# Down projection of a gated conv FFN: the loop over row blocks moved outside the loop over feature slices

## The reference

```
def conv_ffn(x, w_up, conv_w, conv_b, w_down):
    s_len = x.shape[1]
    u = x @ w_up                                        # 1024 -> 2 * 3072
    up = jnp.pad(u, ((0, 0), (CONV_W - 1, 0), (0, 0)))  # causal, width 3
    c = conv_b + sum(up[:, j:j + s_len] * conv_w[j] for j in range(CONV_W))
    gte, val = c[..., :D_FF], c[..., D_FF:]
    return (jax.nn.gelu(gte) * val) @ w_down            # 3072 -> 1024
...
x = layer_norm(ALPHA * x + ffn, ln2_g[l], ln2_b[l])
```

## Time and profile before

| what | value |
|---|---|
| median of 3 runs | 3718.81 us |
| the profiled execution's own time | 3718.81 us |
| its span, first to last instruction | 3716.7 us |
| TensorE (PE) busy | 3423.7 us, 92% |
| VectorE (DVE) busy | 2533.5 us, 68% |
| ScalarE (ACT) busy | 1644.5 us, 44% |
| GpSimd (POOL) busy | 652.1 us, 18% |
| mean granted TensorE clock | 0.964 of full speed |

### The profile page before, as it was taken

One profiled execution on the slowest core, in us unless ns is written; L12 is line 12 of the kernel. 1 busy time (PEld: TensorE's weight loads), 2 busy tenths in 40 slices (PEclk: granted clock), 3 DMA queues, 4 the chain that ended last, 5 costly groups with the idle time before them and its releaser, 6 DMA issues. The chain is left out here.

```text
span 3716.7 us, 40502 instructions
## 1 busy us (share of the span) xinstructions
PE 3423.7 (92%) x15012; PEld 2715.9 (73%) x15064; DVE 2533.5 (68%) x4093; ACT 1644.5 (44%) x2025; POOL 652.1 (18%) x367
## 2 busy tenths in 40 slices
PE   7999899947888999978999799999999999999997
PEld 5788777835555666656777588888888888888886
DVE  5899999967766767636555465567566756666665
ACT  5767777225566666654221133333333333333331
POOL 1022222323455555660000000000000000000000
PEclk9999999978899999999999899999999999999999
DMA  6223322352211111007443433323322333323230
GB/s 166 47 90 102 102 97 90 121 143 53 59 47 44 49 37 44 16 23 238 159 159 102 131 111 116 102 91 123 113 96 102 106 124 102 102 82 114 102 100 33
DMA packets 233022, 356.88 MB, mean 96 GB/s; under 512 B 43453, under 2 KB 150605, under 8 KB 218814
## 3 DMA queue, kind: packets, MB, share of 16 engines
q1 hardware_dynamic: 231774, 349.95, 30.5%
q0 software_dynamic: 1056, 4.36, 0.3%
HBM read 290.13 MB, written 64.13 MB: 95 GB/s over the span
## 5 line engine op out<-in xcount | busy, mean ns | idle before, releaser
L88 PE MATMUL ffn_up<-ffn_xh,ffn_uh 128*128 128x512 f32 x1536 | 599.4, 390 | 9.4 <-DVE ffn_ul L1561 9.4
L90 PE MATMUL ffn_up<-ffn_xh,ffn_ul 128*128 128x512 f32 x1536 | 599.0, 390 | 0.0
L89 PE MATMUL ffn_up<-ffn_xl,ffn_uh 128*128 128x512 f32 x1536 | 598.9, 390 | 0.0
L1519 ACT ACTIVATE ffn_c<-ffn_up,ffn_cb,ffn_cw 128x512 f32<-128x512 f32 x192 | 148.8, 777 | 766.0 <-PE ffn_up L90 760.3
L810 POOL TENSOR_TENSOR att_plo<-att_pf,att_phi 128x1024 fp32r<-128x1024 f32 x168 | 407.7, 2428 | 389.7 <-ACT att_phi L870 389.5
L88 PE MATMUL frt_acc<-frt_xh,frt_wh 128*128 128x512 f32 x864 | 339.6, 393 | 20.3 <-issue 9.4
L88 PEld LDWEIGHTS ffn_up<-ffn_xh,ffn_uh 128*128 128x128 f32 x1536 | 289.2, 188 | 70.6 <-issue 5.2
L89 PE MATMUL frt_acc<-frt_xl,frt_wh 128*128 128x512 f32 x864 | 337.9, 391 | 0.0
L90 PE MATMUL frt_acc<-frt_xh,frt_wl 128*128 128x512 f32 x864 | 337.8, 391 | 0.0
L89 PEld LDWEIGHTS ffn_up<-ffn_xl,ffn_uh 128*128 128x128 f32 x1536 | 289.3, 188 | 59.9
L90 PEld LDWEIGHTS ffn_up<-ffn_xh,ffn_ul 128*128 128x128 f32 x1536 | 289.1, 188 | 60.1
(11 more groups left out here) (267 smaller groups left out, 7482.8 us busy)
## 6 DMA issues: line engine op xcount, KB each, us to landing
ffn_ur<-in_w_up_dram SPq DMA_DIRECT2D x96, 1024.0 KB, 4.8
ffn_dr<-in_w_down_dram SPq DMA_DIRECT2D x64, 768.0 KB, 4.4
zt<-frt_out SPq DMA_DIRECT2D x108, 256.0 KB, 4.3
frt_wr<-in_w_main_dram SPq DMA_DIRECT2D x51, 512.0 KB, 4.2
att_raw<-zt SPq DMA_DIRECT2D x64, 256.0 KB, 4.1
mrg_sg<-zt SPq DMA_DIRECT2D x64, 256.0 KB, 3.6
frt_xr<-in_xt_dram SPq DMA_DIRECT2D x12, 1024.0 KB, 7.8
yt<-att_y SPq DMA_DIRECT2D x32, 256.0 KB, 2.3
```

Of the source, the lines that this page charges most:

```text
L88: pe.matmul(out, ahi, bhi, start=first, stop=False)
L89: pe.matmul(out, ahi, blo, start=False, stop=False)
L90: return pe.matmul(out, alo, bhi, start=False, stop=last)
L1519: act.activation(c[:, k % 2, a, :], up[:, k % 2, a, :], ACT.Identity, scale=cw[:, 2, a, k % NS:k % NS + 1], bias=cb[:, a, k % NS:k % NS + ...
```

## The change

In `fall`, the loop over the four row blocks `b` becomes the outer loop and the loop over the three slices `i` the inner one. The same 36 matmuls are issued, with the same operands and into the same banks, but a bank now gets its nine matmuls in one run. Before, each slice was waited for just before its twelve matmuls. Now one wait for all three slices (`hs` up to `G * (j + 1)`) stands ahead of the first matmul. The wait for the freed bank (`da`) stays ahead of each bank's first matmul, and the count of `dm` after each bank's last one.

```
                 pe.wait_ge(S["dsd"], p + 1)
-                for i in range(G):
-                    pe.wait_ge(S["hs"], G * j + i + 1)
-                    sl = (G * j + i) % R
-                    for b in range(TB):
-                        if p and i == 0:
-                            pe.wait_ge(S["da"], TB * (p - 1) + b + 1)
+                pe.wait_ge(S["hs"], G * (j + 1))
+                for b in range(TB):
+                    if p:
+                        pe.wait_ge(S["da"], TB * (p - 1) + b + 1)
+                    for i in range(G):
+                        sl = (G * j + i) % R
                         last = split3(pe, dn[:, b, :], hh[:, sl, b * P:(b + 1) * P], hl[:, sl, b * P:(b + 1) * P],
                                       dh[:, ch, i, :], dl[:, ch, i, :], i == 0, i == G - 1)
-                        if i == G - 1:
-                            last.then_inc(S["dm"], 1)
+                    last.then_inc(S["dm"], 1)
```

## The result

| | before | changed |
|---|---|---|
| median of 6 runs, us | 3718.35 | 3743.16 |
| lowest to highest, us | 3716.21 to 3719.37 | 3739.35 to 3743.82 |
| ratio, 95% interval | | 1.0065 (1.0052 to 1.0079) |
| the profiled execution's own time, us | 3718.81 | 3739.39 |
| its span, us | 3716.7 | 3737.3 |

The changed kernel is 0.65% slower, 24.8 us at the medians; the prediction was 3740 us (3733 to 3747). The profiled execution was among the fastest of its kernel, 20.6 us above the one before. One run among those of the kernel before that the first four experiments share took 4251.88 us at a mean granted clock of 0.766; no ratio includes it.

A forecast was written before the change was run, and what follows sets the result against it. TensorE was taken to bound the feed-forward stage, so its added idle time delays the end. Pauses 15.5, clock 5.7, first falls 0.1 and seam -0.2 gave 21.1 us on 3718.8, so 3740 us (3733 to 3747).

The forecast's parts named there:

- Falls in the middle cost nothing: Falls inside a part: the third slice is ready 3.8 us early, so the early wait costs nothing.
- First falls of parts 1 to 3: First fall of parts 1, 2 and 3: the wait ends 0.03 us late; 0.1 us for the three together.
- The four pauses: Last group of each part: the first matmul waits for slice 23; 3.66, 3.39, 3.25 and 5.21 us, together 15.5 us.
- The clock: After each pause TensorE's clock runs low: 1.8 us in parts 0, 1 and 3, 0.3 in part 2, together 5.7 us.
- bound of 2.7: Upper bound in us for the clock loss after one pause, from five earlier pauses that lost 1.8 to 2.7 us.
- The total: Whole kernel: 21.1 us added to the profiled execution's 3718.8 us, so 3740 us, 0.57% slower.
- The seam: Between the last two falls: bank 0 is free in time, so the second no longer waits for VectorE's additions; -0.2 us.
- Same bank nine times: Matmuls of the falls, nine in a row into one bank: 0 us expected, bounds 0 and 32 us gained.
- the clock holds: Rival: after the part-end pauses the clock stays up and only the pauses are paid; 3733 us, chance 0.07.
- not in the last alone: Rival: the wait binds only where there are no turns, at the last part's end; 7.0 us, 3726 us, chance 0.02.
- The predicted waits: Sign: four new TensorE waits of `ffn_dn` L88 on `ffn_hl` L1594, three of 3.2 to 3.7 us, one of 5.2.

The follow-up runs named there:

- the first four experiments: Early wait in the old order, new order without the last group, one wait per slice, and filler matmuls in the pauses; their shared kernel before: 3720.25 us.
- The kernel with the new order alone: New loop order with its early wait in groups 0 to 6 (56 of 64 falls), old fall in the last group; 3720.84 us, ratio 1.0001 against the kernel before.
- idle work in both idle times: Changed kernel plus extra matmuls, their result overwritten, in the four pauses and ahead of turn 2 of parts 1 to 3; 3732.74 us, ratio 1.0037.
- the changed kernel's second trace: Changed kernel measured again without further edits, on the same chip as three other kernels; median 3741.82 us, ratio 1.0058 against the kernel before.
- six matmuls ahead of the pause: Changed kernel, but in block 0 each slice is waited for just before its three matmuls; 3729.29 us, ratio 1.0024 against the kernel before.
- Idle work at a fixed count of matmuls: Changed kernel plus 15 (parts 0 to 2) or 22 (part 3) extra matmuls in the four pauses, overwritten afterwards; 3738.58 us, ratio 1.0051.
- the early wait alone: Kernel before, old loop order, with one early wait for all three slices added; 3748.11 us, ratio 1.0068 against the kernel before.

## Why the prediction was right

- **Falls in the middle cost nothing.** Right: the new order in 56 falls measured 1.0001.
- **First falls of parts 1 to 3, 0.1 us together.** Small, and somewhat undersized. The wait is met 0.1 us ahead, but the fall's first matmuls lose some of their pace (TensorE, changed kernel):

```profile
2554.34 0.39 PE L90 MATMUL ffn_up<-ffn_xh,ffn_ul 128*128 128x512 f32 x1
2554.57 0.44 PE L88 MATMUL ffn_dn<-ffn_dh,ffn_hh 128*128 128x512 f32 x1
2554.85 0.39 PE L89 MATMUL ffn_dn<-ffn_dl,ffn_hh 128*128 128x512 f32 x1
```

  0.28 us to the second one; the fall takes 8.25 us from its start to the next rise's, where a fall in the middle of a part takes 8.16, and likewise in the two others: 0.3 us together. The kernel with the new order alone has the same in all three.
- **The four pauses, 15.5 us.** Measured 15.3, each 0.04 to 0.06 us below its own number, since the fall began 0.10 us after `hl` and not 0.14. They could be read from the trace of before because the chain that ends in `hl` contains no work of TensorE's, so it does not move when TensorE waits.
- **The clock, 5.7 us.** Measured 5.9 net of the seam, so 6.1 to 6.2. The mechanism was right: with idle work in both idle times it went. That the sum came so close is in part luck, as the errors in the split cancel: part 3 lost 2.9 us (2.7 net of the seam), above the bound of 2.7 that the five older pauses gave, and part 0 lost 1.35 instead of 1.8.
- **The total.** 3740 us was worked out against a profiled execution, and the traced ones fit: 21.5 us for the stretch in one, 22.1 in the changed kernel's second trace. That second one, 3741.46 us, is 2.1 us above the first, and 1.5 of these it had already lost before the first turn of part 0's end. The median, 3743.16 us, is 3 us above the forecast. None of the runs at 3743 us was traced, so where they spend it stays open; their mean granted clock, 0.961 to 0.963, does not set them apart.
- **The seam, -0.2 us.** Right: 0.23 us where there was 0.32, and the last fall takes 3715.73 - 3707.80 = 7.93 us from its first to its last matmul, where before it was 3695.16 - 3687.10 = 8.06.
- **Same bank nine times.** 0, as said. What the Trainium skill states in "TensorE: Matmul & The Clock Gate", section "A second HAM failure mode: psum-queue depth-cycling", and the prediction weighed, is not what this kernel does: between the part ends falls in either order run at clock 1.00, and a fall takes 8.16 us in both.
- **The rivals.** That the clock holds (3733) is refuted for the changed kernel by the granted clock after its four pauses; with the idle work in both places the clock did hold, and that kernel's median was 3732.74. The wait binds in all four parts, not in the last alone. The predicted waits were there, four of them, though the profile put them down to "issue" and not to `hl`.

## What to carry to other kernels

A wait for several inputs at the head of a run of work costs as much as the latest of them is late, minus nothing: what was ready earlier no longer hides it. Before a loop is turned inside out, compare for every place where it runs, the first and last groups above all, when each input is ready with when the old order first needed it. The price of a pause on the engine that bounds the kernel is its length plus what the clock loses afterwards (here 15.3 us and some 6); and an order that completes outputs one by one pays only where somebody starts on them early, as the last fall did.

## What had not been expected of the hardware

- A low stretch of the clock costs nothing where it lies on work that ends in a wait anyway. With six matmuls ahead of the pause the four part ends cost 9 us by the medians instead of 21 to 25, of which only 5.4 are the 24 matmuls done ahead; in parts 0 to 2 the granted clock was back at 1.00 when the pause ended, and part 3 lost 1.7 us instead of 2.9.
- Idle work at a fixed count of matmuls is no safe filler: when the clock had already dropped, 15 of them took 5.1 us instead of 3.7 and became late themselves.
- After the pause of 5.2 us the granted clock was 0.70 over 10 us (in the traces of the early wait alone and of the changed kernel's second run as well), lower than after any of the five earlier pauses of up to 5.2 us.
